# Activations' high and low halves in one 512-column product, in up and down of the first block

## The reference

```python
def _sq_relu_mlp(h, w_up, w_down):
    u = jax.nn.relu(h @ w_up)          # w_up   1024 x 4096
    return (u * u) @ w_down            # w_down 4096 x 1024

x = x + _sq_relu_mlp(_rmsnorm(x, norm_mlp), w_up, w_down)
```

## Time and profile before

| | |
|---|---|
| median of 3 runs | 1176.24 us (1175.98 to 1176.39) |
| the profiled execution | 1175.98 us |
| its span in the trace | 1174.2 us |
| TensorE matmul busy | 1154.3 us (98% of the span) |
| TensorE weight load busy | 1086.4 us (93%) |
| VectorE busy | 893.1 us (76%) |
| ScalarE busy | 757.8 us (65%) |
| GpSimd busy | 340.5 us (29%) |
| granted TensorE clock | 1.00 of full speed |
| DMA, mean | 185 GB/s |

### The profile page before, as it was taken

The page is one execution under the profiler, slowest core; times in us unless marked ns, Lnnn a source line. Parts: engine busy times, 40 slices in busy tenths (PEclk is TensorE's granted clock), DMA queues, the critical chain, the costliest instruction groups (busy, mean ns, idle before and its releaser), DMA issues.

```text
span 1174.2 us, 26850 instructions
## 1 busy us (share of the span) xinstructions
PE 1154.3 (98%) x9150; PEld 1086.4 (93%) x9150; DVE 893.1 (76%) x1491; ACT 757.8 (65%) x1373; POOL 340.5 (29%) x303
## 2 busy tenths in 40 slices
PE   9999999999999999999999999999999999999998
PEld 8888999999998999999998779999889978999987
DVE  7788777666578877756659979999556776899964
ACT  7766655444565755554557878888556666988852
POOL 3320355300012245522302205555000310455500
PEclk9999999999999999999999999999999999999999
DMA  9554566655655466665654445666745643566673
GB/s 327 176 156 140 178 197 197 197 188 192 215 157 161 147 197 197 198 214 187 203 183 132 139 143 182 197 197 202 228 159 170 241 148 126 187 201 197 202 218 105
DMA packets 64056, 216.64 MB, mean 185 GB/s; under 512 B 7777, under 2 KB 10993, under 8 KB 63985
## 3 DMA queue, kind: packets, MB, share of 16 engines
q1 hardware_dynamic: 63808, 215.17, 56.7%
q10 hardware_dynamic: 176, 0.54, 0.2%
HBM read 211.47 MB, written 1.06 MB: 181 GB/s over the span
## 4 chain that ended last, share of the span: by engine, by line
PE 82%; DVE 10%; ACT 3%; issue 2%; POOL 1%; DMA 1%; SPq 0%; DVEq 0%; POOLq 0%; ACTq 0%
PE bank L785 16%; PE bank L786 16%; PE bank L787 16%; PE bank L712 4%; PE bank L714 4%; PE bank L713 4%; PE bank L661 3%; DVE w_lo L1601 3%; PE bank L663 3%; PE bank L662 3%; PE bank L590 2%; PE bank L591 2%; PE bank L596 1%; PE bank L915 1%; PE bank L932 1%
## 5 line engine op out<-in xcount | busy, mean ns | idle before, releaser
L1601 DVE TENSOR_TENSOR w_lo<-raw,w_hi 128x1024 fp32r<-128x1024 f32 x386 | 505.5, 1318 | 75.1 <-ACT w_hi L1139 73.8
L1139 ACT CAST w_hi<-raw 128x1024 fp32r<-128x1024 f32 x386 | 402.1, 1046 | 239.5 <-PE bank L787 100.9
L785 PE MATMUL bank<-h_hi,w_hi 128*128 128x256 f32 x1184 | 326.9, 276 | 0.4
L786 PE MATMUL bank<-h_lo,w_hi 128*128 128x256 f32 x1184 | 325.6, 275 | 0.0
L787 PE MATMUL bank<-h_hi,w_lo 128*128 128x256 f32 x1184 | 325.6, 275 | 0.0
L785 PEld LDWEIGHTS bank<-h_hi,w_hi 128*128 128x128 f32 x1184 | 227.3, 192 | 1.4 <-DVE h_lo L1675 1.2
L786 PEld LDWEIGHTS bank<-h_lo,w_hi 128*128 128x128 f32 x1184 | 227.3, 192 | 0.1
L787 PEld LDWEIGHTS bank<-h_hi,w_lo 128*128 128x128 f32 x1184 | 227.3, 192 | 0.0
L785 PE MATMUL bank<-a_hi,w_hi 128*128 128x256 f32 x544 | 150.1, 276 | 1.2 <-DVE a_lo L1675 1.1
L786 PE MATMUL bank<-a_lo,w_hi 128*128 128x256 f32 x544 | 149.6, 275 | 0.0
L787 PE MATMUL bank<-a_hi,w_lo 128*128 128x256 f32 x544 | 149.6, 275 | 0.0
(11 more groups left out here) (222 smaller groups left out, 2107.7 us busy)
## 6 DMA issues: line engine op xcount, KB each, us to landing
raw<-in_w_up_sb SPq DMA_DIRECT2D x44, 512.0 KB, 3.4
raw<-in_w_up_fox SPq DMA_DIRECT2D x44, 512.0 KB, 3.5
raw<-in_w_up_a SPq DMA_DIRECT2D x32, 512.0 KB, 3.5
raw<-in_w_down_a SPq DMA_DIRECT2D x32, 512.0 KB, 4.6
raw<-in_w_up_b SPq DMA_DIRECT2D x32, 512.0 KB, 3.4
raw<-in_w_down_b SPq DMA_DIRECT2D x32, 512.0 KB, 4.7
raw<-in_w_in_sb SPq DMA_DIRECT2D x24, 512.0 KB, 3.7
raw<-in_w_in_fox SPq DMA_DIRECT2D x24, 512.0 KB, 3.5
```

Source lines behind the costliest of these rows:

```text
L785: nc.tensor.matmul(dst, w_hi[:, slot, w], in_turns(src_hi[:, at + k, :]), start=begin, stop=False)
L786: nc.tensor.matmul(dst, w_hi[:, slot, w], in_turns(src_lo[:, at + k, :]), start=False, stop=False)
L1139: nc.scalar.copy(w_hi[:, slot, 0:k * P], raw[:, slot, 0:k * P]).then_inc(hi_ready, 1)
L1601: nc.vector.tensor_tensor(w_lo[:, slot, 0:k * P], raw[:, slot, 0:k * P], w_hi[:, slot, 0:k * P].bitcast(f32), ALU.subtract).then_inc(lo_re ...
```

## The change

In the up and down stages of the first block, the product of the high weights takes high and low activations at once, as 512 columns: the sum over high weights by high activations and low weights by high activations stands in columns 0 to 255 of the bank, that over high weights by low activations in columns 256 to 511. Each k-tile then has two products (512 and 256 columns) in place of three (256 each). The two halves of the bank are added at the eviction. In up ScalarE copies the low one to `c_buf2`, VectorE adds the high one into `u_buf`, waits for that, and applies the max and the factor to `u_buf` in place. In down VectorE adds the high half to X, waits for that, and adds the low half. So that one access pattern can reach both, `h2_hi` and `h2_lo` become halves of one tensor, as do `a_hi` and `a_lo`. In the diff the first `before` is ScalarE's in up, then come VectorE's `tile` in down and VectorE's `before` in up.

```diff
-        h2_hi = sb("h2_hi", [P, KT, TOK], f32r)
-        h2_lo = sb("h2_lo", [P, KT, TOK], f32r)
+        h2 = sb("h2", [P, 2, KT, TOK], f32r)
+        h2_hi, h2_lo = h2[:, 0], h2[:, 1]
...
+        WIDE = {"down_a": 0, "down_b": D // P, "up_a": None, "up_b": None}
...
+        def high_and_low(x, k):
+            return x[:, :, k, :].rearrange("p s (h a) -> p s a h", h=2)
+        def low_product(b):
+            return bank[b][:, TOK:2 * TOK].rearrange("p (a h) -> p h a", h=2)
...
+                            if name in WIDE:
+                                both, pair = bank[b][:], high_and_low(a if name in DOWN_OF else h2, at + k)
+                                if begin:
+                                    nc.tensor.matmul(both, w_hi[:, slot, w], pair, start=True, stop=False)
+                                last = nc.tensor.matmul(dst, w_lo[:, slot, w], in_turns(src_hi[:, at + k, :]),
+                                                        start=False, stop=False)
+                                if not begin:
+                                    last = nc.tensor.matmul(both, w_hi[:, slot, w], pair, start=False, stop=end)
+                                continue
...
             def relu(name):
...
+                def before(i, done, b, first):
+                    act.wait_ge(units_done, done)
+                    nc.scalar.copy(halves_of(c_buf2[:, b, :]), low_product(b)).then_inc(low_copied, 1)
...
-            project("up_a", after=relu("up_a"), middle=norm_scale)
+            project("up_a", *relu("up_a"), middle=norm_scale)
...
                 def tile(i, done, b, first):
                     dve.wait_ge(units_done, done)
                     x = halves_of(X[:, i * per + b, :])
-                    nc.vector.tensor_tensor(x, product(b), x, ALU.add).then_inc(tile_out, 1)
+                    nc.vector.tensor_tensor(x, product(b), x, ALU.add).then_inc(high_added, 1)
+                    dve.wait_ge(high_added, i * per + (WIDE[name] + b + 1))
+                    nc.vector.tensor_tensor(x, low_product(b), x, ALU.add).then_inc(tile_out, 1)
...
                 def before(i, done, b, first):
                     dve.wait_ge(units_done, done)
+                    dve.wait_ge(a_ready, i * 4 + (base + b + 1))
+                    dve.wait_ge(low_copied, i * 4 + (base + b + 1))
+                    nc.vector.tensor_tensor(halves_of(u_buf[:, b, :]), product(b), halves_of(c_buf2[:, b, :]),
+                                            ALU.add).then_inc(up_added, 1)
                     dve.wait_ge(rstd_ready, NORMS[name] + 1)
-                    dve.wait_ge(a_ready, i * 4 + (base + b + 1))
-                    nc.vector.scalar_tensor_tensor(halves_of(u_buf[:, b, :]), product(b), 0.0, halves_of(rstd[:]),
-                                                   ALU.max, ALU.mult).then_inc(tile_out, 1)
+                    dve.wait_ge(up_added, i * 4 + (base + b + 1))
+                    nc.vector.scalar_tensor_tensor(u_buf[:, b, :], u_buf[:, b, :], 0.0, rstd[:], ALU.max,
+                                                   ALU.mult).then_inc(tile_out, 1)
```

More of the change, by code:

```diff
@@ L188, in mlp_sb @@
                 return mlp.enter_context(nc.sbuf_tensor(name, shape, dt))
-            a_hi = mlp_sb("a_hi", [P, D_FF // P, TOK], f32r)
-            a_lo = mlp_sb("a_lo", [P, D_FF // P, TOK], f32r)
+            a = mlp_sb("a", [P, 2, D_FF // P, TOK], f32r)
             c_buf2 = mlp_sb("conv_buf", [P, 4, TOK])
             prod = mlp_sb("prod", [P, 2, TOK])
+        a_hi, a_lo = a[:, 0], a[:, 1]
         x_tok = ZM[:].rearrange("p k t -> p (k t)").rearrange("p (a f) -> p a f", a=2)
@@ L302, in build_program @@
         gain_joined = sem("gain_joined")
+        high_added = sem("high_added")
+        low_copied = sem("low_copied")
+        up_added = sem("up_added")
         y_half = sem("y_half")
@@ L1265, in relu @@
             def relu(name):
-                base, first_tile = PRODUCTS[name], plan[name]["tile"]
+                first_tile = plan[name]["tile"]
+                def before(i, done, b, first):
+                    act.wait_ge(units_done, done)
+                    nc.scalar.copy(halves_of(c_buf2[:, b, :]), low_product(b)).then_inc(low_copied, 1)
                 def tile(i, done, b, first):
@@ L1271, in tile @@
                     nc.scalar.activation(a_hi[:, i * 4 + b, :], u_buf[:, b, :], ACT.Square).then_inc(a_hi_ready, 1)
-                return tile
+                return before, tile
             def conv_high(name, i, b):
@@ L1557, in _ @@
             out_projection("out_b", "up_b")
-            project("up_b", after=relu("up_b"), middle=norm_scale)
+            project("up_b", *relu("up_b"), middle=norm_scale)
             join_gains()
```

## The result

The changed kernel takes 1205.35 us (median of 4 runs, 1204.99 to 1205.52), the kernel before, run beside it, 1176.15 us: a ratio of 1.0247 [1.0235, 1.0259], 29.2 us slower. The forecast was 1193.0 us with a range of 1183 to 1201. The time lies 4.35 us above that range. The side and the mechanism came out as forecast; the size didn't, by 12.35 us. The profiled execution has a span of 1203.4 us against 1174.2 us, at a granted clock of 1.00 in both.

A forecast was written before the change was run, and what follows sets the result against it. TensorE was taken to bound the kernel, with VectorE 0.15 us per unit behind in up. Per layer +10.0 (up) - 1.9 (down) + 0.5 (its end) = +8.6 us, 17.2 for both, gave 1193 us, range 1183 to 1201.

The forecast's parts named there:

- Up becomes VectorE's: In up, VectorE's round grows from 2.53 to 2.99 us, over TensorE's 2.62 us per unit, so VectorE sets the pace.
- the copy is hidden: In up, ScalarE's 0.36 us copy ends by 1.4 us after a step, before the next add at 2.5, except tile 0.
- down's gain: In down, TensorE saves 1.9 us per stage, as a k-tile takes 327.6 ns in place of 335.1.
- The wait behind down: At down's end, the next stage's first products wait for the eighth eviction's second add, another 0.46 us each layer.
- Rivals 1: In up, TensorE still sets the pace, with VectorE's round within 2.62 us: faster, 1169 us; chance 6%.
- 2: In up, the add is cheaper, 0.33 us per step: 8 us less, 1185 us; chance 12%.
- 4: In up, VectorE waits for ScalarE's copy in each unit, 0.36 + 0.1 us in 62 rounds: 1221 us; chance 4%.
- 5: Lateness in up is partly absorbed by a shorter start or end, time within 0.2% (2.4 us) of no change; chance 2%.
- rival 3: In up's loops, waits on register values cost 0.12 us more in 48 rounds: 6 us more, 1199 us; chance 15%.
- the round of 2.99 us: VectorE's round in up: the old 2.53 us plus 0.46 us for the add that the next instruction waits for.
- up, lateness of down_a: Down_a's first product waits for up's eviction 30 and starts at about 231.4 in place of 221.45, 10.0 us later.
- Layer b runs the same program: Layer b was taken to lose the same +8.6 us as layer a, 17.2 us for both.

The follow-up runs named there:

- the last run: The changed kernel with the second block's activations in two tensors of their own, g_hi and g_lo, the first block's left joined: 1201.58 us, 1.0217 of the kernel before.

## Why the prediction was wrong, point by point

**Right.** Up becomes VectorE's; the wait for GpSimd stays whole behind the add; the copy is hidden but at tile 0, where the first step was forecast at 143.59 and came at 143.67. TensorE's k-tile takes 0.328 us as forecast, also with the new operand pattern, and down's gain is 1.82 us for 1.9. The wait behind down costs 0.45 us for 0.46. Rivals 1, 2, 4 and 5 are refuted, by rounds of 3.07 us and more, by the add's 0.52 us, by two waits for the copy in all, and by the stages' starts. So is rival 3, below.

**Wrong.** The mechanism was right; what failed are terms of the sum, above all the round of 2.99 us, and the second block, which the sum had at nothing. The forecast's 17.2 us for layers a and b are 12.0 us short of the 29.2 us:

| term | forecast | measured | short by, both layers |
|---|---|---|---|
| up, lateness of down_a | 10.0 | 13.56 | 3.6 |
| up, lateness of down_b | 10.0 | 14.84 | 4.8 |
| down and its end, each layer | -1.4 | -1.4 | 0.1 |
| second block | 0 | 3.5 | 3.5 |

1. *"So a round takes 2.53 + 0.46 = 2.99 us."* Both terms are too small. In the loop the mean round from step 4 to step 28 is (228.66 - 153.78) / 24 = 3.12 us. The add's step is 0.52 or 0.53 us (165.79 to 166.32), not 0.46. A register's value in the wait, rival 3, isn't the reason. At both ends of up the waits have constants, and the step takes 0.52 us there too; in down's loop the wait between the two adds has a register's value, and they are 0.46 us apart:

```profile
234.00 0.42 DVE L1749 TENSOR_TENSOR H<-bank,conv_buf 128x256 f32<-128x256 f32 x1
234.52 0.43 DVE L1753 SCALAR_TENSOR_TENSOR H<-H,rstd 128x256 f32<-128x256 f32 x1
...
245.92 0.42 DVE L1711 TENSOR_TENSOR X<-bank,X 128x256 f32 x1 [2.56 <-PE bank L804]
246.38 0.42 DVE L1713 TENSOR_TENSOR X<-bank,X 128x256 f32 x1
```

Rounds grew by 0.55 us in the loop (2.52 to 3.07) and by 0.53 outside (2.40 to 2.93). What the step in up has and neither down's nor the forget gate's has is a wait instruction of its own ahead of it, since it waits for two semaphores; that this makes the 0.06 us is likely, but no run isolates it. And the old round wasn't 2.53 us: where the loop of up_a turned, the old rounds took 2.75, 2.74 and 2.72 us (161.14, 171.44, 181.73), the others 2.52, which is 2.58 on average. I had measured two rounds that hold no turn. Before the change VectorE's slack hid the turn; now it is paid, 0.23 us in every fourth round. The remaining 0.02 us are the wait for GpSimd, 0.65 for 0.63, and the kernel before with a joined has rounds of 2.54 us too. Over 24 rounds 0.13 us are 3.1 of the 3.6 us; the other 0.5 us are in the rounds at both ends, where each add costs 0.52 as well.
2. *"Layer b runs the same program."* It doesn't: up_b's rounds are 3.15, 3.15, 3.37 and 3.07 us, since the wait that ends at a_lo is 0.72 us there in three of four. That makes 1.3 us more than in up_a, and the joined a makes most of it: put into the kernel before by itself, it lengthens three rounds in four of up_b by 0.06 to 0.08 us, and those of up_a by 0.02.
3. *The joined tensors weren't priced.* The forecast gave a cost to each added instruction and none to the change of a declaration. In the second block it costs 3.5 us in this kernel (3.6 us by the last run, where each version is set against the kernel before beside it) and 4.3 us in the kernel before, by an address that takes VectorE 0.09 us longer once per trip. In up it costs some 0.6 us in layer a and 1.4 us in layer b, an estimate from the rounds of the kernel before with a joined (0.1 and 0.24 us more per trip of four rounds, six trips). So some 5.5 of the 12 us missed are the declaration's; part of it stands in points 1 and 2 already.

## What to carry to other kernels

Where an in-order engine holds a wait in each round, an instruction is dear or free by its place: ahead of the wait the add cost 0.52 us in each round, inside it next to nothing (rounds of 2.55 us for 2.52). Size a round over a whole loop trip, turn included, before you put work on an engine with 0.1 us to spare, since slack hides the turn until the engine becomes the bound. And a declaration isn't free: when a tensor's shape changes, look at the address arithmetic of all loops that index it, in stages that the change doesn't name too.

## What the runs showed of the hardware that I had not expected

- Two engines that share access to SBUF make 0.1 us of phase worth 0.4 us: a_lo took 0.43 us started 0.05 us ahead of GpSimd's product and 0.87 us started 0.05 us behind it. The add from PSUM, which has one operand in SBUF, took 0.42 us beside GpSimd's product, where a_lo, with two, took 0.83. The Trainium skill, "GPSIMD Engine Reference", section "1. Specifications", names contention for VectorE's instructions with two SBUF inputs; these rows agree.
- One instruction and three register operations more for an address cost VectorE 0.09 us once per trip of up_sb (0.66 us for 0.57 from the instruction before), and three more instructions in up_b's loop 0.08 us in each of three rounds.
- Behind a VectorE instruction of 0.42 us the next one starts 0.33 us after its start where it doesn't wait for it, 0.46 us after where it waits, whether on a constant or on a register's value (245.92 to 246.38), and 0.52 us where the program has a wait instruction of its own ahead of it (234.00 to 234.52).
- After a gap TensorE's first product of 256 columns is under way for 0.37 us in place of 0.28, and the next starts 0.21 us behind it in place of 0.11 (759.07 and 759.28): a gap of 0.09 us costs 0.19.
